# Hybrid decoder layer on eight cores: shape registers for the gate/up matmuls, 176 recast weight pieces in place of 120, and DMA transposes in the token sweep

## The chip, the cores and the metric

The kernel runs on all 8 cores of one Trainium2 chip, each core with one sequence of the batch and all the weights. The metric is the device time of the slowest core in microseconds; the median of the runs is compared. The cores do not talk to each other.

## What is computed

One decoder layer on 2048 tokens of width 2048 per core. It has three sub-layers, each added to the residual h, and a final RMSNorm:

- a mixer: RMSNorm, one input projection, then a pooling branch (four trailing windows) and an RWKV-7 branch (16 heads of 64, a recurrence over time), joined by an output projection;
- cross-attention with 4 heads from RMSNorm(h) into 256 memory tokens;
- a mixture of experts: each token picks one of 4 groups and in it 2 of 4 experts.

```python
g_idx = jnp.argmax(g_logits, axis=-1)
top_v, top_i = lax.top_k(e_logits, MOE_TOPK)
top_p = jax.nn.softmax(top_v, axis=-1) * g_w
...
hid = jax.nn.silu(t @ w_gate[e]) * (t @ w_up[e])
out = out + gates[:, e:e + 1] * (hid @ w_down[e])
```

## The kernel before

All operations are first recorded by the helpers of the class `Sched` (`mm`, `act`, `tt`, `stt`, `cp`, `dma` and so on), each with the buffers that it reads and writes and a price in nanoseconds. `schedule` then plans the order of every queue (PE, ACT, DVE, POOL, SP): a list scheduler that takes, on each engine as it comes free, the ready operation with the longest path of prices behind it. A DMA is priced at 2000 ns plus its bytes over `DMA_RATE`. `emit` writes the instructions in that order with semaphore waits. Within a queue the order is fixed from then on: an operation that is late on the chip holds up what stands behind it. Because every instruction comes from a helper, the trace shows the helper's line: L128 is every matmul, L151 every ACT operation, L158 `tt`, L163 `stt`, L172 `ts`, L179 `cp`, L193 every direct DMA.

There are three stages.

**Mixer** (`st_proj`, `st_prep`, `st_solve`, `st_chain`, `st_y`, `pool_piece`, lines 711 to 883). 32 units of one head pair and a quarter of the sequence each run through projection, preparation, a triangular solve and a chain over 8 chunks of 64 tokens. In `st_chain` (829 to 863) every chunk gets its state update and then six matmuls for its output y. `c_steps` (905) computes two products of the attention weights with the memory beside it.

**Token sweep** (lines 984 to 1232). 16 tiles of 128 tokens. For each tile: `d_out` adds the output projection to the residual h (64 matmuls of 512 columns in four blocks), `d_norm` (1154) squares h on ACT for the norm and transposes it by 16 TensorE transposes in f32, whose PSUM results are rounded to bf16 by ACT and DVE in turn into the single buffer hT, `d_scores` (1160) multiplies hT by the key products (2 x 16 matmuls) and exponentiates, `d_mem` (1175) transposes the probabilities, multiplies them by the value products (32 matmuls) and stores h, and `d_route` (1187) transposes h in f32 once more for the router's logits. `d_out` of the next tile and `d_route` of the last one are recorded between these parts. Every second residual add or so releases a recast.

**Experts** (lines 1234 to 1346). The router sorts each group's tokens into 6 buckets, one for each pair of experts, of at most 128 tokens; 24 buckets on a core. Each bucket is gathered, normed and transposed by TensorE (`gather`, 1271). An expert serves the three buckets that hold it: for each of 4 hidden blocks it runs 16 gate and 16 up matmuls over all 3 x 128 = 384 columns (line 1329), whether a bucket's columns are filled or not, then the down projection per bucket.

**Weight pieces and recasts.** The experts' weights are 192 pieces of 128 x 2048, f32 in DRAM. A recast is a DMA on POOL's queue from DRAM to DRAM that rounds a piece to bf16 ahead of time. `ERC` = 30 of every 48 pieces are recast, 120 in all: the first 4 x `EXM` = 56 during the mixer, spread over the chain's steps, and the other 64 in the sweep. In the experts (`piece`, 1295) a recast piece is loaded in bf16 by SP, any other by POOL, cast on the way.

Of the kernel before, what the change touches and what calls it, by code (L numbers as in the profile page):

```python
# [7 lines left out]
F32 = mybir.dt.float32  # L8
BF16 = mybir.dt.bfloat16
I32 = mybir.dt.int32  # L10
AF = mybir.ActivationFunctionType
ALU = mybir.AluOpType
# [11 lines left out]
DMA_RATE = 330.0  # L24
# [36 lines left out]
def fsz(ap):  # L61
    n = 1
    for s in ap.shape[1:]:
        n *= s
    return n


class Sched:
# [38 lines left out]

    def mm(self, items, R=(), W=(), P=(), **kw):
        dur = 10.0
        for it in items:  # L110
            out, lhsT, rhs = it[0], it[1], it[2]
            n, k, m = max(fsz(rhs), 64), lhsT.partition_size(), fsz(lhsT)
            mode = (64 if k <= 64 else 128, 32 if m <= 32 else 64 if m <= 64 else 128)
            if lhsT.dtype == F32 and not (len(it) > 5 and it[5].get("is_transpose")):
                dur += 2.06 * n
            elif mode == (64, 64):
                dur += 0.23 * n
            elif mode == (128, 128):
                dur += max(0.422 * n, 70)
            else:  # L120
                dur += 0.422 * n

        def fn(e, items=items):
            r = []
            for it in items:
                out, lhsT, rhs, st, sp_ = it[:5]
                k = it[5] if len(it) > 5 else {}
                r.append(e.matmul(out, lhsT=lhsT, rhs=rhs, start=st, stop=sp_, **k))  # L128
            return r
        return self.op("pe", fn, dur, R, W, P, mode=mode, **kw)  # L130

# [55 lines left out]
    def dma(self, eng, out, in_, R=(), W=(), P=(), **kw):  # L187
        n = 1
        for s in out.shape:
            n *= s  # L190
        nb = n * sum(4 if a.dtype == F32 else 2 for a in (out, in_) if a.space == "DRAM")
        extra = {k: kw.pop(k) for k in list(kw) if k not in ("after", "bias")}
        return self.op(eng, lambda e: e.dma_start(out=out, in_=in_, **extra), 550.0 if eng == "pool" else 60.0, R, W, P, nbytes=nb, **kw)  # L193

# [19 lines left out]
    def schedule(self):  # L214
# [25 lines left out]
        while left:  # L240
# [49 lines left out]
            for s in o.succ:  # L290
                r = o.end + (LAT if not o.bytes else 0.0)
                if r > s.ready:
                    s.ready = r
                s.n -= 1
                if s.n == 0:
                    heapq.heappush(fut[s.eng], (s.ready, s.i))
# [91 lines left out]
def r3(ap, a):  # L388
    return ap.rearrange("p (a b) -> p a b", a=a)
# [3 lines left out]
EXM, ERC = 14, 30  # L393
# [4 lines left out]
QT = 512  # L398
HS = [slice(0, 64), slice(64, 128)]
# [6 lines left out]
def build(stop=99, fallback=True):  # L406
# [40 lines left out]
    with ExitStack() as es:  # L447
# [6 lines left out]
        CONST_W = 1512  # L454
# [10 lines left out]
        run, tab, idf, idx, flg, flgi = al.f32(24), al.f32(120), al.f32(24), al.f32(24), al.f32(1), al.f32(1)  # L465
        idx.a, flgi.a = idx.a.bitcast(I32), flgi.a.bitcast(I32)
# [362 lines left out]
        def st_chain(u):  # L829
# [5 lines left out]
            hp, chain = U["hp"], chains[U["hp"]]  # L835
            for c in range(8):
# [14 lines left out]
                it = []  # L851
                for h in range(2):
                    y = Y3[HS[h], c, :]
                    if Sp is not None:
                        it.append((y, Sp.a[HS[h], :], A3[HS[h], c, 64:128], True, False))
                    it.append((y, K3[HS[h], c, 0:64], N3[HS[h], c, 64:128], Sp is None, False))
                    it.append((y, V3[HS[h], c, :], K3[HS[h], c, 64:128], False, True))
                it = [it[i] for i in ((0, 3, 1, 4, 2, 5) if Sp is not None else (0, 2, 1, 3))]
                S.mm(it, R=[AR, NB, KB, TV] + ([Sp] if Sp else []), P=[bky])
# [124 lines left out]
        if stop >= 4:  # L984
# [169 lines left out]
            def d_norm(tt):  # L1154
                hb, hq, mxb, st = tl[tt]
                S.act(mxb.a, hb, AF.Square, R=hq, W=[mxb], P=[st], accum_out=st.a[:, 0:1])
                rstd_from(st)
                tposes(hb, hq, r3(hT.a, 16), hT.fresh())
# [75 lines left out]
        if stop >= 5:  # L1234
# [11 lines left out]
            S.cp(flgi.a, flg.a, R=[flg], W=[flgi])  # L1246
            wxr = Ring([S.part(o_, 1024) for o_ in WP[:12]])
# [23 lines left out]
            def gather(b):  # L1271
# [15 lines left out]
                for q in range(4):  # L1287
                    pb = gps_.next()
                    S.mm([(pb.a[:, j * 128:(j + 1) * 128], xn.a[:, (q * 4 + j) * 128:(q * 4 + j + 1) * 128], identb.a, True, True) for j in range(4)],
                         R=[xn, identb], W=[pb])  # L1290
                    for k in range(2):
                        S.cp(dst[k][1][:, q * 4:q * 4 + 4], r3(pb.a, 4), R=[pb], P=[dst[k][0]], eng=("act", "dve")[k])
# [22 lines left out]
            for e in range(16):  # L1315
# [8 lines left out]
                for ffc in range(4):  # L1324
                    pg, pu = eps_.next(), eps_.next()
                    for k, pp in ((0, pg), (1, pu)):
                        w = piece(k, e, ffc)
                        w3 = r3(w.a, 16)
                        S.group([([(pp.a[:, 0:384], w3[:, kc, :], X3[:, kc, :], kc == 0, kc == 15) for kc in range(8 * kk, 8 * kk + 8)], [w, XE[e]]) for kk in range(2)], pp)
# [21 lines left out]
        if stop >= 5 and fallback:  # L1351
# [57 lines left out]
            nc.all_engine_barrier()  # L1409
    return nc  # L1410
# [76 lines left out]
```

## Time and profile before

| | us |
|---|---|
| median of 3 runs | 2524.58 |
| lowest and highest run | 2521.02, 2527.62 |
| the profiled execution's own time | 2513.94 |
| its span (slowest core, core 5) | 2512.3 |
| spans of the eight cores | 2495.1 to 2512.3 |

The page gives the busy time and share of each engine; PE is TensorE's matmuls, PEld its weight loads, which run beside them, and DVE, ACT, POOL and SP are the vector, scalar, GpSimd and sync engines. q0 is the DMA queue of POOL and q1 that of SP; both run on the same 16 DMA engines. The tables further down have their columns named with the group where they aren't plain.

### The profile page before, as it was taken

The numbers are of one execution on the slowest core, as the hardware profiler recorded it, in microseconds if no ns is written. First come the engines' busy times: TensorE is split into PE (matmuls) and PEld (weight loads), VectorE is DVE, ScalarE is ACT, GpSimd is POOL, SyncE is SP. The second block draws the span as 40 slices with busy tenths as digits, with TensorE's granted clock in tenths as the row PEclk, the third lists the DMA queues.
The fourth block names the chain that finished last, engine by engine and source line by source line (L and its number), as shares of the span: only waits on it lengthen the run. The fifth ranks groups of instructions, "written<-read, shape, count | busy, mean of one in ns | idle before, by whom it ended". The sixth has DMA issues, their size and how long they took to land.

```text
span 2512.3 us, 57398 instructions; the slowest of 8 cores (2495.1 to 2512.3 us)
## 1 busy us (share of the span) xinstructions
PE 2277.4 (91%) x25144; PEld 1280.5 (51%) x25144; DVE 1384.6 (55%) x2599; ACT 1238.9 (49%) x2303; POOL 393.5 (16%) x655
## 2 busy tenths in 40 slices
PE   5789999899788899999997999999994999999986
PEld 2355555554455555554554555555552555555543
DVE  3455666677636567676774334343435555666644
ACT  5555776677656676676774323233332232433312
POOL 3122113111130212211000000000001012111111
PEclk9989999999889999999997999999996999999998
DMA  9768567664883868965466676767765788999973
GB/s 217 98 108 119 93 108 108 110 114 80 143 126 94 116 114 126 136 113 96 88 138 171 160 137 152 146 154 145 152 124 187 178 242 224 243 241 258 251 210 114
DMA packets 183805, 372.80 MB, mean 148 GB/s; under 512 B 80992, under 2 KB 134752, under 8 KB 169856
## 3 DMA queue, kind: packets, MB, share of 16 engines
q0 software_dynamic: 100560, 217.45, 52.5%
q1 hardware_dynamic: 82992, 151.64, 18.9%
q8 instruction: 199, 3.26, 0.5%
q14 instruction: 54, 0.44, 0.1%
HBM read 510.79 MB, written 121.77 MB: 252 GB/s over the span
## 4 chain that ended last, share of the span: by engine, by line
PE 77%; DMA 11%; DVE 5%; ACT 4%; issue 2%; POOL 1%; POOLq 0%; DVEq 0%
PE ps L128 77%; ACT big L151 4%; DMA big<-w_lo 3%; DVE big L158 3%; DVE big L163 2%; DMA big<-w_kv 1%; DMA big<-x 1%; DMA big<-wg_l 1%; DMA out<-big 1%; DMA big<-w_qT 1%; DMA qkd<-big 1%; POOL big L193 1%; DMA big<-h_s,big 1%; DMA big<-mem 1%; DMA vod<-big 0%
## 5 line engine op out<-in xcount | busy, mean ns | idle before, releaser
L128 PE MATMUL ps<-big 64*64 64x64 bf16 (+6 forms) x25144 | 2277.4, 262 | 212.0 <-ACT big L151 68.3
L128 PEld LDWEIGHTS ps<-big 64*64 64x64 bf16 (+3 forms) x25144 | 1280.5, 109 | 1208.4 <-issue 147.5
L151 ACT ACTIVATE big<-ps 128x512 bf16<-128x512 f32 (+2 forms) x904 | 505.7, 588 | 810.8 <-PE ps L128 794.7
L158 DVE TENSOR_TENSOR big<-ps,big 128x512 bf16<-128x512 f32 (+3 forms) x656 | 465.4, 721 | 439.8 <-PE ps L128 312.1
L151 ACT ACTIVATE big<-big 128x512 f32<-128x512 f32 (+9 forms) x896 | 541.2, 634 | 256.6 <-DVE big L158 107.3
L151 ACT ACTIVATE big<-ps,big 128x512 f32<-128x512 f32 (+3 forms) x332 | 211.4, 649 | 184.8 <-PE ps L128 181.4
L163 DVE SCALAR_TENSOR_TENSOR big<-ps,big 128x512 f32<-128x512 f32 (+2 forms) x316 | 223.6, 721 | 138.3 <-ACT big L151 83.6
L163 DVE SCALAR_TENSOR_TENSOR big<-big 128x512 bf16<-128x512 f32 (+4 forms) x212 | 227.7, 1078 | 35.3 <-DMA big<-h_s,big 19.2
L158 DVE TENSOR_TENSOR big<-big 128x512 bf16<-128x512 f32 (+11 forms) x406 | 200.2, 511 | 30.2 <-ACT big L151 24.2
L163 DVE SCALAR_TENSOR_TENSOR big<-big,ps 128x64 f32<-128x64 f32 (+1 forms) x280 | 92.6, 331 | 168.3 <-PE ps L128 166.3
L179 DVE CAST big<-ps 128x512 bf16<-128x512 f32 x168 | 110.8, 684 | 60.2 <-ACT big L151 45.1
L193 POOL DMA_DIRECT2D big<-w_kv x128 | 68.2, 539 | 156.5 <-PE ps L128 155.0
L1171 DVE RECIPROCAL big<-big 128x4 f32<-128x4 f32 x16 | 2.8, 176 | 142.9 <-ACT big L151 142.8
L193 POOL DMA_DIRECT2D wdc<-wd_l x40 | 19.8, 494 | 313.9 <-PE ps L128 149.7
L193 POOL DMA_DIRECT2D wgc<-wg_l x40 | 19.8, 495 | 278.8 <-PE ps L128 123.6
L179 DVE COPY big<-ps 128x512 f32<-128x512 f32 (+3 forms) x57 | 27.4, 502 | 64.2 <-PE ps L128 62.2
L193 POOL DMA_DIRECT2D wuc<-wu_l x40 | 19.9, 496 | 267.7 <-DVE big L163 77.4
L1309 POOL DMA_INDIRECT out<-big x24 | 35.6, 1482 | 97.4 <-DVE big L163 95.3
L193 POOL DMA_DIRECT2D big<-w_lo x48 | 36.1, 767 | 79.7 <-PE ps L128 70.0
L193 POOL DMA_DIRECT2D big<-wu_l x24 | 13.3, 553 | 212.2 <-PE ps L128 212.2
L193 POOL DMA_DIRECT2D big<-w_qT x64 | 34.1, 539 | 78.6 <-PE ps L128 76.9
L193 POOL DMA_DIRECT2D big<-w_rkv x48 | 26.2, 546 | 120.5 <-PE ps L128 113.8
(27 smaller groups left out, 309.8 us busy)
## 6 DMA issues: line engine op xcount, KB each, us to landing
big<-x SPq DMA_DIRECT2D x32, 1024.0 KB, 7.5
big<-w_rkv POOLq DMA_DIRECT2D x48, 512.0 KB, 8.9
wuc<-wu_l POOLq DMA_DIRECT2D x40, 512.0 KB, 7.5
wgc<-wg_l POOLq DMA_DIRECT2D x40, 512.0 KB, 7.4
wdc<-wd_l POOLq DMA_DIRECT2D x40, 512.0 KB, 7.3
big<-wuc SPq DMA_DIRECT2D x40, 512.0 KB, 9.7
big<-wgc SPq DMA_DIRECT2D x40, 512.0 KB, 7.5
big<-wdc SPq DMA_DIRECT2D x40, 512.0 KB, 8.9
```

The source lines that it names most:

```text
L128: r.append(e.matmul(out, lhsT=lhsT, rhs=rhs, start=st, stop=sp_, **k))
L151: return self.op("act", lambda e: e.activation(out=out, in_=in_, func=func, **kw), dur, R, W, P, tbl=TBL.get(func))
L158: return self.op(eng, lambda e: e.tensor_tensor(out=out, in0=a, in1=b, op=op), dur, R, W, P, after=after)
L163: return self.op(eng, lambda e: e.scalar_tensor_tensor(out=out, in0=a, scalar=s, in1=b, op0=op0, op1=op1), dur, R, W, P)
L179: return self.op(eng, lambda e: e.tensor_copy(out=out, in_=a), dur, R, W, P)
L193: return self.op(eng, lambda e: e.dma_start(out=out, in_=in_, **extra), 550.0 if eng == "pool" else 60.0, R, W, P, nbytes=nb, **kw)
L1171: S.op("dve", lambda e, st=st: e.reciprocal(out=st.a[:, 8:12], in_=st.a[:, 4:8]), 100.0, R=[st], P=[st])
L1309: S.op("pool", lambda e: e.indirect_dma_start(out=out, out_offset=IOA(ap=idx.a[:, b:b + 1], axis=0), in_=y.a, in_offset=None, bounds_check ...
```

## The change

- **Gate and up.** After the router, the largest of each expert's three bucket counts is taken, clipped to 1 to 128 and put as the middle size of a shape (128 columns step, 3 buckets) into one of 16 shape registers of TensorE. Of each 16 gate or up matmuls the first and the last still run over 384 columns, the 14 between them over 3 x that count.
- **Recasts.** `ERC` goes from 30 to 44 (176 pieces), `EXM` from 14 to 24 (96 of them in the mixer, 80 in the sweep).
- **Sweep.** `d_norm` squares into hT instead of the mixer tile's buffer, rounds h once to bf16 on DVE into that buffer, and transposes it by one DMA from SP into hT; the 16 TensorE transposes and their four evacuations go. `d_route` keeps its own.
- **Chain.** The y matmuls of two chunks go out together.
- **Planner.** A matmul that follows a matmul counts as ready at once, `DMA_RATE` is 320, a DMA's bytes are counted by its larger side, and three prices are changed.

```diff
-DMA_RATE = 330.0
+DMA_RATE = 320.0
...
-    def mm(self, items, R=(), W=(), P=(), **kw):
-        dur = 10.0
+    def mm(self, items, R=(), W=(), P=(), pre=None, **kw):
+        dur = 10.0 if pre is None else 2500.0
...
-            n, k, m = max(fsz(rhs), 64), lhsT.partition_size(), fsz(lhsT)
+            kw5 = it[5] if len(it) > 5 else {}
+            n, k, m = kw5.get("cols", max(fsz(rhs), 64)), lhsT.partition_size(), fsz(lhsT)
...
-                dur += 2.06 * n
+                dur += (0.52 if "tile_position" in kw5 else 2.06) * n
...
+                if "shape" in k:
+                    k.pop("cols")
+                    sr = k.pop("shape")
+                    out, rhs = out.shape_from_register(sr), rhs.shape_from_register(sr)
...
-        nb = n * sum(4 if a.dtype == F32 else 2 for a in (out, in_) if a.space == "DRAM")
+        nb = n * max(4 if a.dtype == F32 else 2 for a in (out, in_))
...
+    def dmat(self, out, in_, R=(), W=(), P=()):
+
+        return self.op("sp", lambda e: e.dma_start_transpose(out, in_), 60.0, R, W, P, nbytes=128 * fsz(in_) * 2.6)
...
-                r = o.end + (LAT if not o.bytes else 0.0)
+                r = c + d if e == "pe" and s.eng == "pe" else o.end + (LAT if not o.bytes else 0.0)
...
-EXM, ERC = 14, 30
+EXM, ERC = 24, 44
...
+YB = 2
...
-                it = []
-                for h in range(2):
-                    y = Y3[HS[h], c, :]
...
+                ys_.append((c, Sp))
+                if c % YB == YB - 1:
+                    it = []
+                    for c_, Sq in ys_:
...
+                    S.mm(it, R=[AR, NB, KB, TV] + [Sq for _, Sq in ys_ if Sq], P=[bky])
+                    ys_ = []
...
             def d_norm(tt):
                 hb, hq, mxb, st = tl[tt]
-                S.act(mxb.a, hb, AF.Square, R=hq, W=[mxb], P=[st], accum_out=st.a[:, 0:1])
+                S.act(hT.a, hb, AF.Square, R=hq, W=[hT], P=[st], accum_out=st.a[:, 0:1])
                 rstd_from(st)
-                tposes(hb, hq, r3(hT.a, 16), hT.fresh())
+
+                S.cp(mxb.a, hb, R=hq, W=[mxb])
+                S.dmat(r3(hT.a, 16), mxb.a, R=[mxb], W=[hT])
...
+            S.red(n4[:, :, 0], r6[:, :, 0:3], ALU.max, R=[run], P=[nmx])
+            for i, (a, b, c) in ((1, (0, 3, 4)), (2, (1, 3, 5)), (3, (2, 4, 5))):
+                S.tt(n4[:, :, i], r6[:, :, a], r6[:, :, b], ALU.max, R=[run], P=[nmx])
+                S.tt(n4[:, :, i], n4[:, :, i], r6[:, :, c], ALU.max, R=[run, nmx], P=[nmx])
+            S.ts(nmi.a, nmx.a, 128.0, ALU.min, 1.0, ALU.max, R=[nmx], W=[nmi])
...
+            def shapes(e):
+                regs = [es.enter_context(e.register(f"nm{i}")) for i in range(16)]
+                one, w128, three = [es.enter_context(e.register(n)) for n in ("c1", "c128", "c3")]
+                r = [e.load(regs, nmi.a[0:1, :])]
+                for rg, v in ((one, 1), (w128, 128), (three, 3)):
+                    e.reg_mov(rg, v)
+                for i in range(0, 16, 4):
+                    r.append(e.move_shape([e.shape_register(j) for j in range(i, i + 4)], [[(one, regs[j]), (w128, three), (one, one), (one, one)] for j in range(i, i + 4)]))
+                return r
...
-                         R=[xn, identb], W=[pb])
+                         R=[xn, identb] + ([nmi] if (b, q) == (1, 0) else []), W=[pb] + ([shp] if (b, q) == (1, 0) else []), pre=shapes if (b, q) == (1, 0) else None)
...
-                        S.group([([(pp.a[:, 0:384], w3[:, kc, :], X3[:, kc, :], kc == 0, kc == 15) for kc in range(8 * kk, 8 * kk + 8)], [w, XE[e]]) for kk in range(2)], pp)
+
+                        sh = dict(shape=nc.tensor.shape_register(e), cols=300)
+                        S.group([([(r3(pp.a[:, 0:384], 3), w3[:, kc, :], r3(X3[:, kc, :], 3), kc == 0, kc == 15, sh if kc % 15 else {}) for kc in range(8 * kk, 8 * kk + 8)],
+                                  [w, XE[e], shp]) for kk in range(2)], pp)
```

## Rows read from the trace of the kernel before

**Rows 1.** The page, part 1: busy us, share of the span, instructions.

```profile
PE 2277.4 (91%) x25144; PEld 1280.5 (51%) x25144; DVE 1384.6 (55%) x2599; ACT 1238.9 (49%) x2303; POOL 393.5 (16%) x655
```

**Rows 2.** Table by stretches, one core: busy us (instructions) of each engine, then clock, DMA share, GB/s.

```profile
core 5: us, PE busy (x) PEld busy (x) DVE busy (x) ACT busy (x) POOL busy (x), PEclk, DMA share, GB/s
0.00:1390.00 1390.00, 1234.13 (x18749) 706.63 (x18750) 849.34 (x1699) 901.51 (x1677) 262.63 (x474) 0.95 0.70 120
1450.00:1850.00 400.00, 400.00 (x2494) 213.93 (x2492) 146.10 (x368) 121.40 (x263) 24.83 (x51) 1.00 0.68 143
1890.00:2000.00 110.00, 75.62 (x494) 44.72 (x493) 55.73 (x110) 21.48 (x39) 13.28 (x14) 0.80 0.58 183
2050.00:2450.00 400.00, 379.93 (x2271) 212.44 (x2269) 232.27 (x279) 122.14 (x195) 65.29 (x85) 0.98 0.90 240
```

**Rows 3.** PE by line and shape, 1900 to 2512 us: count | busy us, mean ns | idle before.

```profile
L128 PE MATMUL ps<-big 128*128 128x384 bf16 x2048 | 349.1, 328 | 4.7 <-DVE big L163 2.8 <-ACT big L151 1.6 <-DMA big<-wg_l 0.3
```

**Rows 4.** PE by line and shape, 1450 to 1850 us.

```profile
L128 PE MATMUL ps<-big 128*128 128x512 bf16 x1556 | 345.3, 379 | 0.0
L128 PE MATMUL ps<-big 128*128 128x128 f32 x384 | 48.6, 273 | 0.0
```

**Rows 5.** DMA, 2100 to 2400 us: SP's queue, and its issues with median us to landing.

```profile
q1 hardware_dynamic: 9634, 35.11, 34.3%
...
big<-wdc SPq DMA_DIRECT2D x24, 512.0 KB, 9.8
big<-wuc SPq DMA_DIRECT2D x23, 512.0 KB, 10.0
big<-wgc SPq DMA_DIRECT2D x21, 512.0 KB, 7.9
```

**Rows 6.** DMA, 1450 to 1850 us: POOL's queue, and issues with median us to landing.

```profile
q0 software_dynamic: 1646, 26.74, 41.1%
...
h_s<-big SPq DMA_DIRECT2D x12, 1024.0 KB, 11.6
big<-x SPq DMA_DIRECT2D x11, 1024.0 KB, 7.5
wdc<-wd_l POOLq DMA_DIRECT2D x18, 512.0 KB, 8.0
wgc<-wg_l POOLq DMA_DIRECT2D x17, 512.0 KB, 7.6
wuc<-wu_l POOLq DMA_DIRECT2D x16, 512.0 KB, 8.0
```

**Rows 7.** Waits of PE, 0 to 1390 us: us in total, times, longest us.

```profile
PE ps L128 <- DMA big<-w_kv: 10.7, 11, 3.5
```

**Rows 8.** DVE by line and shape, 1450 to 1850 us.

```profile
L172 DVE TENSOR_SCALAR big<-big 128x256 bf16<-128x256 f32 x48 | 14.5, 348 | 0.4
```

**Rows 9.** Timeline of DVE, 1564 to 1587 us: start us, us, instruction, idle before.

```profile
1566.10 0.69 DVE L158 TENSOR_TENSOR big<-ps,big 128x512 f32<-128x512 f32 x1 [1.26 <-PE ps L128]
```

**Rows 10.** Timeline of ACT, 1564 to 1587 us.

```profile
1566.83 1.91 ACT L151 ACTIVATE big<-big 128x2048 bf16<-128x2048 f32 x1 [1.86 <-DVE big L158]
...
1581.83 0.47 ACT L151 ACTIVATE big<-ps,big 128x256 f32<-128x256 f32 x1 [4.17 <-PE ps L128]
```

**Rows 11.** PE by line and shape, 1573.2 to 1578.1 us.

```profile
L128 PE MATMUL ps<-big 128*128 128x512 bf16 x16 | 3.8, 379 | 0.0
L128 PE MATMUL ps<-big 128*128 128x128 f32 x16 | 2.1, 275 | 0.0
```

**Rows 12.** Timeline of SP's queue, 1556 to 1592 us.

```profile
1568.86 0.53 SPq L193 DMA_DIRECT2D big<-mixd  x1
```

**Rows 13.** The tile mixd on SP, 1450 to 1850 us: its loads to landing.

```profile
DMA to landing us min/median/max: 5.5/10.5/18.0
```

**Rows 14.** Timeline of POOL, 1556 to 1592 us.

```profile
1567.08 0.49 POOL L193 DMA_DIRECT2D wdc<-wd_l  x1 [17.00 <-DVE big L158]
1568.81 0.49 POOL L193 DMA_DIRECT2D wgc<-wg_l  x1 [1.24 <-DVE big L158]
```

## What the change does to the time: a prediction

> **What bounds the kernel now.** I read the page's first part, then the table by stretches. PE is busy 91% of the span, far above DVE and ACT [rows 1]. The stretches show three stages [rows 2]. The mixer (to about 1390 us) has PE busy 89% at a granted clock of 0.95, with 156 us of PE idle. The token sweep has PE busy every microsecond from 1450 to 1850 at clock 1.00. The expert stage has PE busy 95% between 2050 and 2450, with the DMA engines at 0.90. So in the last two stages a microsecond off PE is a microsecond off the end, as long as nothing takes PE's place; the candidates are the DMA engines in the experts and one landing per tile in the sweep. All sums are made against the profiled execution (its time 2513.9, its span 2512.3). That run lies 10.6 us under the median 2524.6; I add this back at the end. A change of 0.3% (7.6 us) is about the least that a measurement of this kernel can tell from none.
>
> **Gate and up.** 2048 matmuls of 384 columns take 349.1 us, 0.1705 us each [rows 3]; 512 columns take 345.3/1556 = 0.2219 us [rows 4]. The slope is 0.0514/128 = 0.40 ns a column. The change leaves the first and the last of each sixteen at 384 and gives 14 of 16, 1792 in all, three times the expert's largest bucket. The router of the reference, worked out on its own inputs, gives largest buckets of 72 to 124 tokens, in the mean 94 to 98 on each core, 96.5 over the eight: 289 columns. That saves 95 x 0.40 = 38 ns on each, 1792 x 0.038 = **68 us**; the core with the most has 293 columns and saves 65, the one with the least 281 and 74. No row shows a matmul that fetches its shape from a register. If fetching costs as much as the columns give back, nothing is saved; that is the lower end. I take the full saving, because the nearest row, the same matmul, follows its columns.
>
> **Setting the registers** puts 16 loads, 19 moves and 4 shape moves on PE once, between the second bucket's transposes, and some ten tiny DVE instructions ahead of it. No row has them. The stretch has PE busy 76 of 110 us [rows 2] for want of gathered tokens, which hides them; without that cover I put 5 us. I take **+2**.
>
> **Recasts.** 120 become 176, so 56 weight pieces come as plain bf16 loads instead of casting ones. A plain piece costs the 16 DMA engines 0.343 x 300 us / 68 = 1.5 us [rows 5]. A recast costs 0.411 x 400 us / 51 = 3.2 us [rows 6], and I price a casting load, with the same bytes in, the same. In the experts the DMA engines lose 56 x 1.7 = 95 us of work. This is what lets PE gain there. In the inner 400 us they do 360 us of work [rows 2]; PE would want only 352 us after the cut, so without the recasts the engines would be over-full. With them it is 292 of 352, a share of 0.83. I leave **+2** for loads that come late at moments. The price is paid earlier: 40 more recasts in the mixer are 128 us of DMA work, share 0.70 to 0.79, and 16 more in the sweep are one more per tile.
>
> **Mixer.** Its y matmuls go out in pairs of chunks and the planner's prices move (PE to PE without a pause, DMA by the larger side, rate 320), so every queue's order may shift, with no matmul removed. Of PE's 156 us of idle time there the waits for w_kv, the largest for a DMA, are 10.7 us [rows 7]. What a new order gives I bound by a tenth of that idle time, -15; what 40 more recasts in POOL's queue, ahead of the weight loads, take I bound by three times the w_kv wait, +30. I take **0**: no row favours either.
>
> **Sweep, what goes.** Per tile 16 transposes of 128x128 f32, 48.6/384 = 0.127 us each [rows 4], all on a PE that is never idle: 256 x 0.127 = **-32 us**. With them go two evacuations on ACT and two on DVE per tile.
>
> **Sweep, what comes.** DVE gets one rounding of 128x2048 a tile. It has no row; eight of the 128x256 scalings to bf16, 8 x 0.348 = 2.8 us, are an upper bound [rows 8], and one alone, 0.3 us, a lower. DVE is busy 146 of 400 us [rows 2], and ACT's squaring (1.91 us) runs beside it, so I cost it at nothing; without that cover it is 0.9 us a tile. The new step is the transfer. Squaring now writes its discarded result into hT, so the transpose waits for squaring and rounding, and the scores wait for its landing. Take one tile. Its residual is complete at 1566.8 us [rows 9]; squaring ends at 1568.74, and the first scores reach ACT at 1581.83 [rows 10], so 16 matmuls of 0.222 us put the scores' start at 1578.2. In between PE works on other things for 11.4 us, the last 4.9 us of it 16 matmuls of the next tile and the 16 transposes [rows 11]. Without the transposes 9.4 us are left. The transfer can be issued at 1568.9, where the mixd load goes now [rows 12], so a landing of up to 7.3 us is hidden, and each further microsecond stops PE in each of 16 tiles. If the planner sends only one group of 8 ahead, 5.6 us are hidden.
>
> How long the landing is, no row shows. The nearest is the mixd load, with the same 512 KB in the same stretch: 5.5/10.5/18.0 us [rows 13]. The x load takes 7.5, the recasts 7.6 to 8.0, the h2 store 11.6 [rows 6]. I take 9, the middle of these medians: the transfer needs no DRAM, but it starts amid recasts, two of which go out within 2 us of it [rows 14]. The stall is 1.7 us, 16 x 1.7 = **+27**; the ends are 0 (landing 5.5) and +171 (18.0). The sweep comes to -5. The Trainium skill ("DMA: Bandwidth & Descriptors", Latency and other measured facts) gives a DMA transpose 261 GB/s; by it my estimate is 2.0 us of transfer, which with little waiting would land inside the cover and make the whole sum -96 (the first rival); no row here shows one. Behind the transpose on SP stand the h2 store and the loads two tiles ahead. The mixd load now waits for it and moves from 1568.9 to about 1578; with 10.5 us to land it is there at 1588, and its first matmul comes after 1600. DMA work per tile (1556/128 = 12.2 tiles in 400 us, 32.9 us each, share 0.68) goes from 22.4 to about 28 us with a recast and 1.5 to 3.2 us for the transfer: full, but not over.
>
> **Sum.** -68 +2 +2 +0 -32 +27 = -69: 2513.9 - 69 = 2445; with the 10.6 us back, **2456 us**.
>
> **The rivals.**
> *The transposes land early.* They move within SBUF, and some loads there land in 5.5 us. Then the stall is 0 and the sum -96: 2429. Against it stands the burst of recasts. Chance 0.2.
> *The transposes land late, and PE waits for them in every tile* (the other side). It speaks for it that the nearest row's maximum is 18.0, and that a fifth recast per tile falls into the same adds. The Trainium skill ("DMA: Bandwidth & Descriptors", Queues, rings and completion order) has each DMA engine take turns between queues packet by packet, so that a transfer of many packets would queue behind a recast with each; no row shows the packets of a transpose. At a landing of 16 the stalls are 16 x 8.7 = 139: the sum is +43, 2568. It decides from where 16 x (landing - 7.3) eats 96, at 13.3 us. Such stalls would show as idle gaps before the scores and perhaps a granted clock under 1.00 in the sweep. Chance 0.13.
> *The mixer pays for the recasts*, +30: 2486. For: more casting traffic in the queue of its weights; against: DMA waits are a small part of PE's idle time now. Chance 0.1.
> *The register shape does not shorten the matmul* (the change doesn't do what it says): the sum is -1, 2524. Against: plain short matmuls follow their columns. Chance 0.07.
>
> **Numbers.** The forecast has 0.5; its own range is 2429 to 2480 (landings from 7.3 to 10.5). To hold 8 in 10 I reach down to 2405 (early landing with a small gain in the mixer) and up to 2520 (the mixer's rival, and landings to about 13). Faster by over 0.3%: forecast, early landing, mixer and a little of the register case, 0.83. Same: 0.05, most of it the register case. Slower: 0.12, the late landing.
>
> **What would show it.** In the changed profile the gate/up matmuls should take about 0.13 us in 14 of 16, the experts' stage should shrink by 60 to 70 us with a DMA share near 0.83, and the sweep's period be 31 to 34 us. Wrong would be: a PE that waits for the transpose by over 4 us a tile, gate/up still at 0.17 us, PE waits for DMA in the mixer that double, or PE waits for weight pieces in the experts.

## The result, and the profile of the changed kernel

The changed kernel is **slower**: the ratio of its time to that of the kernel before is 1.0595, 95% interval [1.0537, 1.0652]. (Its median of 2743.47 us holds executions on a disturbed die, which the ratio leaves out.) The profiled execution took 2682.57 us, against 2513.94 before. The forecast was 2456.

Line numbers have moved by five: a matmul is now L133, an ACT operation L156, `tt` L163, `stt` L168, `ts` L177, `cp` L184, a direct DMA L198; the transposing DMA is L202. I cut each core's trace into three stages: the mixer ends with the last 64x64 matmul, the sweep with the first gather, the experts with the span. Medians of the eight cores, lowest and highest in brackets:

| us | mixer | sweep | experts | median core's span | slowest core's |
|---|---|---|---|---|---|
| before | 1365.8 (1359 to 1379) | 534.5 (534 to 536) | 602.3 (597 to 604) | 2503.3 | 2512.3 |
| changed | 1429.1 (1392 to 1464) | 664.4 (625 to 693) | 526.5 (522 to 543) | 2622.9 | 2681.0 |

So the experts gained 76 us, the mixer lost 63 and the sweep 130: +117 on a middle core. The rest of the +169 in time is spread: the cores now end 98 us apart, not 17, and the slowest counts.

The page's first part and its chain of the changed kernel (beside [rows 1]):

```profile
PE 2243.1 (84%) x24888; PEld 1272.0 (47%) x24892; DVE 1385.5 (52%) x2591; ACT 1225.1 (46%) x2277; POOL 394.9 (15%) x655
...
PE 60%; DMA 25%; ACT 6%; DVE 5%; issue 3%; POOL 1%; SPq 0%; POOLq 0%; DVEq 0%
```

PE is busy 34 us less, at a lower granted clock (0.911 on this core, against 0.957 on the slowest core before), and a quarter of the chain that ended last is DMA. The table by stretches, to be read against [rows 2] (columns as there):

```profile
0.00:1390.00 1390.00, 1203.29 (x17757) 684.04 (x17758) 815.56 (x1629) 862.03 (x1597) 281.12 (x511) 0.92 0.78 123
1450.00:1850.00 400.00, 300.35 (x1689) 145.38 (x1687) 101.39 (x218) 76.35 (x174) 27.34 (x48) 0.87 0.84 133
2200.00:2600.00 400.00, 384.03 (x2631) 242.94 (x2630) 270.98 (x330) 151.45 (x234) 47.40 (x47) 0.99 0.83 270
```

The sweep, in which PE never paused, has PE idle a quarter of the time, and the granted clock fell from 1.00 to 0.87. The experts pass 2631 matmuls in 400 us instead of 2271, at the DMA share that was forecast, 0.83. Who ends PE's waits in the sweep (us in total, times, longest), and what the DMA issues took to land there, 1500 to 2050 us (x issues, KB, median us):

```profile
PE ps L133 <- DMA big<-big: 141.1, 12, 31.1
PE ps L133 <- ACT big L156: 8.4, 8, 1.8
```

```profile
q0 software_dynamic: 2085, 33.95, 44.4%
q1 hardware_dynamic: 58027, 38.67, 36.9%
...
h_s<-big SPq DMA_DIRECT2D x12, 1024.0 KB, 12.3
big<-x SPq DMA_DIRECT2D x12, 1024.0 KB, 7.7
...
big<-mixd SPq DMA_DIRECT2D x13, 512.0 KB, 6.8
big<-big SPq DMA_TRANSPOSE x13, 20.3
```

`big<-big` by DMA is the transpose. It lands after 20.3 us, where 9 was forecast. One tile shows how that becomes idle time: the timelines of SP, then of PE (start, duration, instruction, idle before it):

```profile
1617.04 9.60 SPq L202 DMA_TRANSPOSE big<-big  x1
1626.69 2.61 SPq L198 DMA_DIRECT2D h_s<-big  x1
1635.27 0.53 SPq L198 DMA_DIRECT2D big<-mixd  x1
```

```profile
1614.73 10.12 PE L133 MATMUL ps<-big 128*128 128x512 bf16 x87
1635.30 5.30 PE L133 MATMUL ps<-big 128*128 128x512 bf16 x12 [10.45 <-DMA big<-big]
```

The transpose is issued at 1617.04; PE runs dry at 1624.85, so 7.8 us were covered; the transfer lands 18.2 us after its issue, and the scores start then. Issuing alone held SP for 9.6 us.

PE by form in the experts, beside [rows 3]; a matmul with its shape from a register is shown as 128x0:

```profile
L133 PE MATMUL ps<-big 128*128 128x0 bf16 x1792 | 258.5, 289 | 0.0
...
L133 PE MATMUL ps<-big 128*128 128x384 bf16 x256 | 75.3, 327 | 2.6 <-DVE big L168 1.9 <-ACT big L156 0.7
L133 PE MATMUL ps<-big 128*128 128x128 bf16 x392 | 35.3, 232 | 33.4 <-DVE big L168 21.4 <-issue 8.1 <-DVE big L184 3.1
```

One such matmul is 39 ns shorter than a 384-column one was (328 ns). The busy times of the two forms can't be added, since neighbours of different forms overlap; from one start to the next the median was 163 ns on every core before and is 118 to 130 now.

### The profile page after: what moved, and what is told of

It is laid out like the page before. It is cut to its first block, busy times and chain, and to the rows that moved or that the text cites. A ratio compares the mean times of both kernels' runs of the same rounds, so it can differ in the third digit from the quotient of the medians.

```text
span 2681.0 us, 56989 instructions; the slowest of 8 cores (2583.3 to 2681.0 us)
## 1 busy us (share of the span) xinstructions
PE 2243.1 (84%) x24888; PEld 1272.0 (47%) x24892; DVE 1385.5 (52%) x2591; ACT 1225.1 (46%) x2277; POOL 394.9 (15%) x655
## 4 chain that ended last, share of the span: by engine, by line
PE 60%; DMA 25%; ACT 6%; DVE 5%; issue 3%; POOL 1%; SPq 0%; POOLq 0%; DVEq 0%
PE ps L133 60%; DMA big<-big 10%; ACT big L156 5%; DMA big<-w_lo 3%; DVE big L163 2%; DMA big<-w_kv 2%; DMA big<-h_s,big 2%; DVE big L168 2%; DMA h_s<-big 1%; DMA big<-x 1%; DMA qkd<-big 1%; DMA big<-w_qT 1%; DMA out<-big 1%; DMA vod<-big 1%; POOL big L198 1%
## 5 line engine op out<-in xcount | busy, mean ns | idle before, releaser
L133 PE MATMUL ps<-big 64*64 64x64 bf16 (+7 forms) x24888 | 2243.1, 263 | 413.6 <-DMA big<-big 141.9
L133 PEld LDWEIGHTS ps<-big 64*64 64x64 bf16 (+2 forms) x24888 | 1271.6, 110 | 1376.4 <-issue 230.5
L163 DVE TENSOR_TENSOR big<-ps,big 128x512 bf16<-128x512 f32 (+3 forms) x656 | 464.9, 721 | 622.6 <-PE ps L133 464.9
L156 ACT ACTIVATE big<-ps 128x512 bf16<-128x512 f32 (+2 forms) x872 | 487.4, 587 | 623.1 <-PE ps L133 603.3
L156 ACT ACTIVATE big<-big 128x512 f32<-128x512 f32 (+6 forms) x896 | 543.1, 632 | 307.5 <-DVE big L163 126.7
L156 ACT ACTIVATE big<-ps,big 128x512 f32<-128x512 f32 (+3 forms) x332 | 211.2, 648 | 502.8 <-PE ps L133 500.0
L168 DVE SCALAR_TENSOR_TENSOR big<-ps,big 128x512 f32<-128x512 f32 (+2 forms) x316 | 221.6, 719 | 108.9 <-ACT big L156 75.2
L168 DVE SCALAR_TENSOR_TENSOR big<-big 128x512 f32<-128x512 f32 (+4 forms) x212 | 227.6, 1078 | 35.6 <-DMA big<-h_s,big 24.4
L163 DVE TENSOR_TENSOR big<-big 128x512 bf16<-128x512 f32 (+11 forms) x412 | 201.4, 507 | 38.3 <-ACT big L156 33.4
L168 DVE SCALAR_TENSOR_TENSOR big<-big,ps 128x64 f32<-128x64 f32 (+1 forms) x280 | 92.6, 331 | 185.5 <-PE ps L133 182.4
L184 DVE CAST big<-ps 128x512 bf16<-128x512 f32 x136 | 90.5, 684 | 52.8 <-ACT big L156 22.9
L198 POOL DMA_DIRECT2D big<-w_kv x128 | 68.1, 539 | 163.3 <-PE ps L133 160.1
L198 POOL DMA_DIRECT2D wuc<-wu_l x64 | 33.5, 523 | 384.7 <-PE ps L133 98.0
L198 POOL DMA_DIRECT2D wgc<-wg_l x48 | 24.8, 517 | 388.8 <-DVE big L163 125.2
L198 POOL DMA_DIRECT2D wdc<-wd_l x64 | 34.2, 534 | 297.3 <-DVE big L163 113.4
L184 DVE COPY big<-ps 128x512 f32<-128x512 f32 (+3 forms) x57 | 27.7, 503 | 49.7 <-PE ps L133 26.6
L1316 POOL DMA_INDIRECT big<-h_s,big x24 | 26.4, 1100 | 152.3 <-DMA out<-big 86.8
L198 POOL DMA_DIRECT2D big<-w_lo x48 | 36.2, 773 | 82.7 <-PE ps L133 73.1
L198 POOL DMA_DIRECT2D big<-w_rkv x48 | 26.4, 550 | 129.9 <-PE ps L133 122.6
```

The source lines that it names most:

```text
L156: return self.op("act", lambda e: e.activation(out=out, in_=in_, func=func, **kw), dur, R, W, P, tbl=TBL.get(func))
L163: return self.op(eng, lambda e: e.tensor_tensor(out=out, in0=a, in1=b, op=op), dur, R, W, P, after=after)
L168: return self.op(eng, lambda e: e.scalar_tensor_tensor(out=out, in0=a, scalar=s, in1=b, op0=op0, op1=op1), dur, R, W, P)
L184: return self.op(eng, lambda e: e.tensor_copy(out=out, in_=a), dur, R, W, P)
L1316: S.op("pool", lambda e: e.indirect_dma_start(out=y.a, out_offset=None, in_=h2_s, in_offset=IOA(ap=idx.a[:, b:b + 1], axis=0), bounds_chec ...
```

## The experiments

Stages as above, medians of the eight cores, worked out from the traces; "time" is the profiled execution's, and the ratio is against the kernel before on the same chip. "Landing" is the transposes' median, then the time that the slowest tenth exceeds and the maximum, over all cores; the trace has no landing for some (in the changed kernel it has 83 of 128, in e5 112), and those are left out.

| run | mixer | sweep | experts | time | landing |
|---|---|---|---|---|---|
| before | 1365.8 | 534.5 | 602.3 | 2513.94 | |
| changed | 1429.1 | 664.4 | 526.5 | 2682.57 | 15.4, 26, 49 |
| e1 | 1435.1 | 549.8 | 534.9 | 2542.59 | |
| e2 | 1378.4 | 657.9 | 601.1 | 2690.18 | 13.4, 25, 31 |
| e3 | 1420.6 | 551.1 | 530.3 | 2527.27 | |
| e4 | 1376.3 | 535.1 | 601.8 | 2523.41 | |
| e5 | 1379.0 | 558.0 | 684.8 | 2636.68 | 5.7, 8, 32 |
| e6 | 1375.9 | 642.5 | 601.6 | 2672.26 | 11.7, 25, 31 |
| e7 | 1373.0 | 534.5 | 587.0 | 2506.22 | |
| e8 | 1413.0 | 555.7 | 538.0 | 2526.23 | |
| e9 | 1377.2 | 568.8 | 603.2 | 2562.54 | 10.0, 25, 30 |
| e10 | 1376.1 | 642.6 | 569.3 | 2617.34 | |
| e11 | 1350.7 | 534.5 | 689.1 | 2591.94 | |
| e12 | 1372.4 | 534.6 | 583.9 | ratio 0.9956 [0.9932, 0.9979] | |
| e13 | 1444.8 | 616.2 | 533.8 | 2638.12 | 6.2, 18, 80 |
| e14 | 1446.4 | 605.9 | 531.2 | 2608.4 | 6.2, 15, 50 |
| e15 | 1378.8 | 554.8 | 590.9 | ratio 1.0081 [1.0052, 1.0111] | 10.8, 19, 44 |
| e16 | 1381.8 | 543.2 | 588.4 | ratio 1.0018 [0.9988, 1.0049] | 13.9, 19, 23 |
| e17 | 1380.3 | 533.3 | 588.8 | ratio 0.9965 [0.9945, 0.9985] | 12.7, 16, 19 |

**Which part costs what.** e1 is the changed kernel with TensorE's transposes; e2 to e4 are the kernel before with one part alone: the DMA transposes; the shapes with all recasts; the planner and the pairs.

```diff
# e1, against the changed kernel
-                S.act(hT.a, hb, AF.Square, R=hq, W=[hT], P=[st], accum_out=st.a[:, 0:1])
+                S.act(mxb.a, hb, AF.Square, R=hq, W=[mxb], P=[st], accum_out=st.a[:, 0:1])
...
-                S.cp(mxb.a, hb, R=hq, W=[mxb])
-                S.dmat(r3(hT.a, 16), mxb.a, R=[mxb], W=[hT])
+                tposes(hb, hq, r3(hT.a, 16), hT.fresh())
# e2, against the kernel before: these lines the other way round
# e3, against e1
-DMA_RATE = 320.0
+DMA_RATE = 330.0
...
-                dur += (0.52 if "tile_position" in kw5 else 2.06) * n
+                dur += 2.06 * n
...
-                r = c + d if e == "pe" and s.eng == "pe" else o.end + (LAT if not o.bytes else 0.0)
+                r = o.end + (LAT if not o.bytes else 0.0)
...
-YB = 2
+YB = 1
# e4, against e1: EXM, ERC = 14, 30, and gate/up at 384 columns
```

> The changed kernel with the 16 TensorE transposes per tile put back; recasts, shapes, planner and chain pairs as changed. Theory A (the sweep's loss is the transfer's late landing): the sweep, mixer's end to first gather, falls from 625 to 693 us back to about 535 on every core, the experts stay near 525 to 540 us, the mixer stays at 1392 to 1464 us, and the time is near 2520 us. Rival (16 more recasts in the sweep, or the planner's prices, cost it): the sweep stays above 600 us.

> The kernel before with the rounding and the DMA transpose alone; 64 recasts in the sweep, old planner prices, no shapes, no pairs. Theory A: the mixer stays at 1359 to 1379 us and the sweep is 600 us or more, since four recasts a tile hold the transfer up nearly as five do; the time is 2590 us or more. Rival (the transfer is late only with the fifth recast and the new plan): the sweep is within 20 us of 535 and the time near 2525 us.

> The kernel before with the shape registers and the 176 recasts (96 of them in the mixer) alone; TensorE transposes, old planner prices, no pairs. Theory B (the mixer's 30 to 85 us are the price of 40 more recasts): the mixer is 1390 us or more here too. Rival C (they come from the planner's prices or the pairs): the mixer is back at 1360 to 1380 us, and with the experts 70 us shorter the time is near 2455 us.

> The kernel before with the planner's prices and the pairs of chunks alone; 120 recasts, no shapes, TensorE transposes. Theory B: the mixer stays at 1360 to 1380 us and the time near 2525 us. Rival C: the mixer is 1390 us or more and the time 2550 us or more.

The DMA transposes alone lengthen the sweep by 123 us (e2), and taking them out of the changed kernel gives 115 back (e1). The shapes with all recasts take 72 us off the experts, and the recasts hand them back: +55 in the mixer, +17 in the sweep (e3). Planner and pairs alone leave sweep and experts as they were (e4); the mixer is 10 us longer, but so it is in e2, e5, e6 and e9, which don't touch it. A new order is not the reason. In e7 and e12 each queue holds, through the mixer and the sweep, the same instructions in the same order as in the kernel before, as far as the trace's names and shapes tell, and their mixer is 7 us longer all the same. What all these runs share is the changed kernel's layout of SBUF (1544 words of constants in place of 1512); and the kernel before has one trace only. Which of the two it is, no run shows.

**What delays the transfer.** e5 is e2 without recasts in the sweep; e6 is e2 with each recast split by rows.

```diff
# e5
-EXM, ERC = 14, 30
+EXM, ERC = 14, 14
# e6, both places
-                    S.dma("pool", d_, s_, P=[bs], after=[o])
+                    S.dma("pool", d_.rearrange("(a b) n -> b a n", b=16), s_.rearrange("(a b) n -> b a n", b=16), P=[bs], after=[o])
```

> The DMA transpose alone, as in the run before it, but only the mixer's 56 recasts are made (ERC 14) and none in the sweep; 64 more pieces are cast by POOL in the experts. Theory D (the transfer is late because recasts share the DMA engines with it): it lands in 8 us or less, and the sweep is 500 to 520 us, below the 535 of TensorE transposes. Rival E (the transpose itself is slow beside any loads and stores, or its issue is): it lands in 10 us or more still and the sweep stays over 580 us. The experts get longer, to 620 us or more.

> The DMA transpose alone, with all 120 recasts, but each recast walks its piece in single rows of 4 KB in an order that can't be merged, in place of 16 pieces of 32 KB; bytes and count the same. Theory D1 (a DMA engine gives a recast piece of 32 KB 3.2 us at a time, and the transfer waits for many of them): landing falls to 8 us or less and the sweep to 560 us or less. Theory D2 (the recasts' bytes or the DMA share as such hold it up): landing and sweep stay as they were, 13.7 us and about 658 us.

DMA of e2, of e5 and of e6 from 1450 to 1850 us (queues: packets, MB, share; then median us to landing):

```profile
q0 software_dynamic: 1216, 19.93, 34.2%
q1 hardware_dynamic: 41573, 29.19, 33.6%
...
big<-mixd SPq DMA_DIRECT2D x9, 512.0 KB, 5.2
big<-big SPq DMA_TRANSPOSE x10, 15.2
```

```profile
q1 hardware_dynamic: 52560, 36.28, 32.4%
...
big<-mixd SPq DMA_DIRECT2D x11, 512.0 KB, 4.5
big<-big SPq DMA_TRANSPOSE x12, 5.6
```

```profile
q0 software_dynamic: 5665, 20.61, 37.0%
...
big<-big SPq DMA_TRANSPOSE x10, 17.2
```

Without recasts the transpose lands nearly as fast as a plain load of the same bytes (5.6 beside 4.5 us); with them it takes 15.2. So it is the recasts.

The mixd load's 5.2 us in e2 is no fair comparison with that: it stands behind the transpose on SP and often starts when the recasts are done. Over all cores of e2, by the recasts in flight at the issue or issued within the next 4 us (one without a landing in the trace is counted with the core's median):

| recasts | 0 | 1 | 2 |
|---|---|---|---|
| transpose, median us | none | 10.1 | 13.8 |
| mixd load, median us | 5.1 | 6.1 | 10.0 |

Both move as 2048 packets of 256 bytes. So recasts delay the load too, and the transpose by some 4 us more. A recast's data go in 16 packets of 32 KB in e2 and in 128 of 4 KB in e6; that leaves the landing about where it was (17.2 here; 11.7 against 13.4 over all cores). Even so the quiet sweep (e5) takes 558 us, not the 502 that 16 x 2 us less would give. PE there, by stretches, and one tile of its timeline:

```profile
1450.00:1850.00 400.00, 377.06 (x2252) 193.20 (x2290) 147.92 (x363) 104.48 (x230) 0.00 (x0) 1.00 0.33 92
```

```profile
1605.61 1.56 PE L133 MATMUL ps<-big 128*128 128x128 bf16 x36 [1.33 <-ACT big L156]
1607.33 5.26 PE L133 MATMUL ps<-big 128*128 128x512 bf16 x25 [0.16 <-issue]
1613.00 24.59 PE L133 MATMUL ps<-big 128*128 128x512 bf16 x122 [0.41 <-DMA big<-big]
```

Gaps of 2 us a tile stand where the f32 transposes had filled PE. The first of these waits for ACT, which empties PSUM only after its squaring (timeline of ACT in the same tile):

```profile
1603.06 1.91 ACT L156 ACTIVATE big<-big 128x2048 bf16<-128x2048 f32 x1 [6.47 <-DVE big L163]
...
1604.97 1.55 ACT L156 ACTIVATE big<-ps 128x512 f32<-128x512 f32 x3
```

The last tile adds a stall of its own; its transpose stands behind the first loads for the experts on SP (timeline of SP in e5):

```profile
1865.63 0.80 SPq L198 DMA_DIRECT2D big<-wgc  x2
1866.47 0.44 SPq L198 DMA_DIRECT2D big<-wuc  x1
1872.14 24.24 SPq L202 DMA_TRANSPOSE big<-big  x1
```

**The recasts' price.** e7, and e12 in more rounds, are e3 with the 120 recasts of before; e8 is e3 with recasts by rows (as e6); e10 and e11 move the number.

```diff
# against e3
-EXM, ERC = 24, 44
+EXM, ERC = 14, 30    # e7, e12
+EXM, ERC = 14, 38    # e10
+EXM, ERC = 0, 16     # e11
```

> The kernel before with the shape registers alone: 120 recasts, TensorE transposes, old planner and no pairs. If the experts needed the 56 recasts, as the prediction has it (DMA work of 360 us in 352), they shrink by 30 to 50 us only, from 602 to about 560 us. Rival: the loads run ahead far enough and the experts shrink by the full 70 us. Mixer 1366 and sweep 535 us either way; time 2450 to 2490 us.

> Shape registers and 176 recasts with TensorE transposes and the old planner, each recast in rows of 4 KB. Theory F1 (the mixer pays for the time of one 32 KB piece, during which everything else on that engine waits): the mixer falls from 1420 back to 1385 us or less and the time to about 2470 us. Theory F2 (it pays for the recasts' share of the DMA engines): the mixer stays at 1410 us or more.

> Shapes with 152 recasts, 56 in the mixer and 96 in the sweep (six a tile); TensorE transposes, old planner, no pairs. Theory I (a recast costs about what it saves, 1.0 us, wherever it is put): the sweep grows from 535 to 560 to 570 us, the experts fall from 587 to about 555 us, the time stays within 10 us of 2506. Rival J (the sweep, with DMA engines at 0.68, has room): the sweep stays under 545 us and the time is near 2480 us.

> Shapes with 64 recasts, all in the sweep and none in the mixer; TensorE transposes, old planner, no pairs. Theory I (about 1.2 us for each recast in the mixer, from the first one on): the mixer falls from 1373 by 50 to 70 us to about 1310 us, the experts grow from 587 by 55 to 75 us, the time is within 15 us of 2506. Rival K (the mixer has room for the first 56 and only the further 40 hurt): the mixer stays over 1355 us and the time is 2545 us or more.

> The shape registers alone once more, timed: 120 recasts, TensorE transposes, old planner, no pairs. By the one look at it (mixer 1373, sweep 535, experts 587 us) 12 to 20 us faster than the kernel before, a ratio of 0.992 to 0.995. Rival: no difference, 0.997 to 1.003.

Experts from 2050 to 2450 us in e3 and in e7, and a wait of PE in e7's experts:

```profile
2050.00:2450.00 400.00, 379.55 (x2621) 243.06 (x2620) 267.09 (x325) 157.92 (x240) 49.70 (x48) 0.98 0.85 267
```

```profile
2050.00:2450.00 400.00, 343.48 (x2234) 210.95 (x2234) 231.22 (x277) 122.48 (x193) 64.47 (x83) 0.93 0.92 236
```

```profile
PE ps L133 <- DMA big<-wdc: 15.7, 4, 6.8
```

With 120 recasts the DMA engines are at 0.92, PE idles 57 of 400 us and passes as few matmuls as before (2234): the shapes alone bring the experts 15 to 18 us of the 72, less than either theory had. They are still, with e17, the best version, 0.4% faster than the kernel before. What one more recast saves in the experts and costs ahead of them, from the table:

| recasts | saved in the experts | cost ahead |
|---|---|---|
| mixer 0 to 56 (e11 to e7) | 102/56 = 1.8 us each | mixer 22/56 = 0.4 |
| 40 more in the mixer, 16 in the sweep (e7 to e3) | 57/56 = 1.0 | mixer 48/40 = 1.2; sweep 17/16 = 1.0 |
| sweep 64 to 96 (e7 to e10) | 18/32 = 0.6 | sweep 108/32 = 3.4 |

The packets' size changes little here too (e8). Neither theory had the sixth recast a tile right, which is over the edge (643 us, where 570 was the most expected); nor did the mixer of e11 fall to 1310 us, or stay over 1355. PE waits of e10 in the sweep, and the landing of its mixd loads (min/median/max):

```profile
PE ps L133 <- DMA big<-mixd: 114.8, 5, 25.1
```

```profile
DMA to landing us min/median/max: 7.2/19.1/62.5
```

**The planner's price and the last tile.** `dmat` was priced at 4.1 us, so the planner put its followers where PE would wait. e9 is e2, and e13 the changed kernel, with 16 us in its place; e14 is e13 with the last tile transposed by TensorE; e15 is e7 with DMA transposes at that price in 15 tiles and TensorE's in the last.

```diff
-        return self.op("sp", lambda e: e.dma_start_transpose(out, in_), 60.0, R, W, P, nbytes=128 * fsz(in_) * 2.6)
+        return self.op("sp", lambda e: e.dma_start_transpose(out, in_), 60.0, R, W, P, nbytes=14000 * DMA_RATE)
...
+                if tt == NTT - 1:
+                    S.act(mxb.a, hb, AF.Square, R=hq, W=[mxb], P=[st], accum_out=st.a[:, 0:1])
+                    rstd_from(st)
+                    tposes(hb, hq, r3(hT.a, 16), hT.fresh())
+                    return
```

> The DMA transpose alone, with 120 recasts, but the planner is told that a transpose lands after 16 us in place of 4. Theory G (the fault is the plan: it puts too little work ahead of the scores, and 16 us could be covered in a tile of 33): the sweep falls from 658 to 570 us or less. Rival H (there is no more work to put ahead, since PSUM banks and the one hT buffer tie the order): the sweep stays at 630 us or more.

> The changed kernel in full, only with the transpose priced at 16 us for the planner in place of 4.1. Theory G (the plan is what failed: the landing can be covered): the sweep falls from 664 to 600 us or less, the time from 2682 to 2600 us or less. Rival L (five recasts a tile and the transposes over-fill the DMA engines, as six recasts without transposes do, and no order mends that): the sweep stays at 640 us or more.

> As the one before, and the last tile keeps its TensorE transposes, since there the transfer stands behind the experts' first loads on SP (24 us to issue, 30 to land). Theory M (the last tile alone costs some 25 us): the sweep is another 20 to 30 us shorter than in the run before. Rival: the difference is under 10 us, since PE has nothing else to do there anyway.

> A version meant to beat both: shape registers, 120 recasts, old planner and no pairs, the DMA transpose priced at 16 us in 15 tiles and TensorE transposes in the last. If both theories hold the sweep is 505 to 545 us (535 with TensorE transposes), the experts 585, the mixer 1373, and the ratio to the kernel before 0.98 to 1.00. Rival (the transposes still hold the scores up now and then): the sweep is over 550 us and the ratio over 1.00.

The price of 16 us takes 89 us off e2's sweep (e9) and 48 off the changed kernel's (e13), there less than the theory had; the last tile another 10 (e14), half of what was expected. Not all of this is work put ahead of the scores: in the new order the transposes also meet fewer recasts, and the median landing falls from 13.4 to 10.0 us in e9 and from 15.4 to 6.2 in e13. Counted as in the table for e2, 76 of the changed kernel's 128 transposes have three or more recasts about, and 18 of e13's. No run parts the two effects. With four recasts a tile the sweep is still 20 us over TensorE's (e15). What is left in e13 is the tail: on core 2 one transpose took 80 us, and the recasts and stores issued in the 30 us after it took 60 to 70. Its issue on SP, and the DMA engines' busy tenths and GB/s in 40 slices from 1560 to 1660 us:

```profile
1568.61 29.07 SPq L202 DMA_TRANSPOSE big<-big  x1
```

```profile
DMA  9495968699999991999959992992354955957422
GB/s 296 96 406 140 216 83 132 60 45 16 17 39 16 16 17 29 118 28 44 36 34 58 46 42 40 82 53 40 12 53 60 112 83 201 321 125 188 104 99 84
```

In seven slices, from 1580 to 1597 us, the DMA engines are shown as 90% busy and move 16 to 45 GB/s. Over the sweeps of all cores, the slices of 2.5 us at 90% or more and under 50 GB/s number 35 in the changed kernel and 23 each in e2 and e13. There are none in the kernel before, e3 and e10, which have recasts and no DMA transposes, and none in e5, which has the transposes and no recasts there. So it takes both.

**Recasts behind the landing.** e16 is e15 with a tile's recasts released by its first exponential of the scores, once the transpose has landed; e17 is e16 with 10 us as the price.

```diff
# e16: the same call, at another place
-                while (nj[1] - len(ejobs)) * 120 < nj[0] * nj[1] and ejobs:
+                while (nj[1] - len(ejobs)) * 15 < nj[0] * nj[1] and ejobs:
...
-                    recast(S.ops[-1])
...
+                        if h == 0:
+                            recast(S.ops[-1])
# e17, against e16
-nbytes=14000 * DMA_RATE
+nbytes=8000 * DMA_RATE
```

> The kernel before with the shape registers (30 pieces of 48 recast, 14 x 4 in the mixer, y one chunk at a time), and the sweep's transposes by DMA, priced at 16 us in the planner, the last tile's by TensorE; new: a tile's recasts go out only after its first scores' exponential, when the transpose has landed, and no longer at the residual adds. Beside e15 this tells whether it is recasts in flight during the transfer that delay it. Theory (they are): median landing at most 8 us in place of 10.8, sweep 505 to 540 us in place of 554.8, ratio below 1.000. Rival (recasts later collide with other loads, and a transfer that lands early only turns into idle time elsewhere in the tile): landing may fall, sweep at least 545 us, ratio at least 1.003.

> e16 with the transpose priced at 10 us in the planner in place of 16. Theory (recasts in flight are the delay): the transfer now lands in less than 8 us, so a shorter price costs nothing and the sweep is within 8 us of e16's or shorter. Rival (landing stays 10 us or more): the order planned for 10 us lets PE run dry, sweep at least 15 us longer than e16's.

Split. The median landing did not fall (13.9 and 12.7 us), against the theory; but its tail did (maximum 44 us in e15, 23 and 19 here). The sweep came down to 543 us in e16, short of the 540 that the theory had as its most, and to 533 in e17, and the shorter price was the better one. Two tiles of e17 show both: SP's timeline, and the recasts on POOL:

```profile
1602.06 6.42 SPq L202 DMA_TRANSPOSE big<-big  x1
...
1633.39 1.90 SPq L202 DMA_TRANSPOSE big<-big  x1
```

```profile
1622.85 0.97 POOL L198 DMA_DIRECT2D wuc<-wu_l  x2 [31.12 <-ACT big L156]
1623.81 0.97 POOL L198 DMA_DIRECT2D wdc<-wd_l  x2
1624.76 0.49 POOL L198 DMA_DIRECT2D wuc<-wu_l  x1
```

The five recasts go out together, and the last lands at 1647.9, 14.5 us into the next transpose, which lands at 1649.6. A tile's copies take most of its 31 us, so no place is free of them. But now each tile is alike. The 96 transposes of e17 whose landing the trace has, by the number of recasts in flight at the issue or issued within the next 4 us:

| recasts | 0 | 1 | 2 | 3 | 4 | 5 |
|---|---|---|---|---|---|---|
| transposes | 14 | 9 | 25 | 22 | 22 | 4 |
| median landing, us | 4.5 | 9.6 | 11.9 | 13.5 | 14.7 | 19.0 |

Recasts without a landing in the trace (236 of the run's 960) are not counted here; counted with the core's median they leave 4.5, 9.6, 9.9, 13.5, 13.7 and 18.9. On average each recast goes with some 3 us more. PE waits 4.5 us in all for it in e17's sweep, and 27 us in all, the rest for ACT and DVE:

```profile
PE ps L133 <- ACT big L156: 10.7, 9, 1.4
PE ps L133 <- DVE big L184: 6.7, 10, 2.4
PE ps L133 <- DMA big<-big: 4.5, 5, 1.2
```

That is nearly all of the 32 us of transposes taken off PE, and the sweep is where it was. e17 and e12 can't be told apart.

## Why the prediction was wrong

**The step that failed is the landing**: "I take 9, the middle of these medians". It was 13.4 us with the recasts of before and 15.4 with the new ones, 25 and more in a tenth of the tiles. The sum's other end, "+171 (18.0)", was nearer. The nearest row was fair in bytes and packets and still too low: with two recasts about, the mixd load lands after 10.0 us in e2 and the transpose after 13.8. The cover was right (7.3 forecast, 7.8 in the tile shown), and so was the rule built on it: the late rival "decides at 13.3 us", and it came. Its formula, taken over the changed kernel's recorded landings one by one, gives 154 us of stalls, less 32 the sweep +122; e1 has 115. For e2 it gives +84, where 123 was measured, so it holds in sign and rough size only.

The landing is not the whole miss: with TensorE's transposes the changed kernel (e1) still takes 2542.59 us, where the kernel before took 2516.5 on the same chip. Most of the rest is in the two terms for the recasts, below.

**"-32" for the transposes** did not come either, where the landing was hidden: the quiet sweep was 24 us longer than with TensorE, of which the last tile's stall is 21 (e5), and the best 1 us shorter (e17). PE was "never idle" because these transposes filled it while ACT and DVE finished; taken out, the gaps opened.

**"DMA work per tile ... full, but not over"**, by which the fifth recast cost nothing: it cost 15 to 17 us (e1, e3), and the sixth another 92 (e10 against e3).

**Mixer "0: no row favours either"**, with +30 as its bound: it measured +63, of which the 40 recasts are 48 (e3 against e7, which has the same layout) to 55 (against the kernel before). The w_kv waits on which the bound stood grew only from 10.6 to 17.5 us (mean of the cores, before and e3); PE waits for ACT rose by 10, issue gaps by 17, DVE by 3, and PE's busy time by 16, at a granted clock of 0.940 in the mixer against 0.954. So the loss is spread over many small waits and does not come from one load; how, stays open.

**Right** were gate/up (38 ns forecast, 39 read), the experts' need for recasts (DMA at 0.92 without them, 0.83 with), and the experts as a whole (-64 forecast, -72 in e3). "+2" for setting the registers was 8.1 us, in one gap on PE (the issue wait among the forms above). DVE's rounding at no cost held; it takes 1.2 us.

**Confidence.** The late landing had 0.13 though its condition, 13.3 us, lay within the row's own 5.5 to 18.0, beside a median of 10.5. A step with no row and such a spread should have had near even chances.

The Trainium skill ("Advanced Engine Details and Errata", X-Bar Transpose (TRN2)) has transposing DMAs as fast as regular ones. Without recasts the traces nearly agree (5.6 beside 4.5 us); beside two recasts they don't (13.8 beside 10.0). The Trainium skill's rule of turns between queues, packet by packet ("DMA: Bandwidth & Descriptors", Queues, rings and completion order), fits the 3 us for each recast, if the trace's packets are those of the rule. By the traces a transpose has 2048 packets, 128 for each of the 16 engines if they are spread evenly, and a recast one of 32 KB for each, which takes 3.1 us (median in e2's sweep). In its 128 turns the transpose would let each recast in flight pass once, and not "a recast with each" packet. In e6 a recast has eight packets of 4 KB for each engine, of 0.32 us: nearly the same sum, so e6 does not speak against the rule. This is argued from counts. It explains neither the extra 4 us beside a load nor the slow tail, and their cause stays open.

## What to carry to other kernels

Work moved from a full engine to the DMA engines has to be priced with the traffic that is there when it starts; measure it alone with that traffic and without, and look at its slow tail, since a fixed order of queues pays for the slowest. A list scheduler's price for a new transfer is part of the change: here a price of 16 us in place of 4.1 was worth 48 to 89 us, in part because the new order let transposes and recasts meet less. Bytes brought forward (the recasts) have a marginal price in every stage that takes them, and the last ones cost more than they save.

## What was not expected of the hardware

- A transpose of 512 KB lands in 4.5 us with no recast about and, on average, some 3 us later for each one in flight (e17's table); issuing it holds SP for up to 39 us in the changed kernel, and with it the stores and loads behind.
- DMA engines shown as 90% busy that move 16 to 45 GB/s, for 17 us, with one transpose and recasts in flight (e13). Such slices came only in runs that have both.
- A matmul whose shape comes from a register follows its columns (118 to 130 ns from start to start, 163 at 384 columns) and costs nothing per instruction that can be seen.
